# A two-part transformer kernel: sigmoids before a weight copy, a pool mixer on padded buffers, retention products in another order, four banks drained before their second step

## The chip, the core and the metric

The kernel runs as one program on one core of a Trainium2 chip. The core has TensorE (PE, matrix products, with weight loads shown as PEld), VectorE (DVE), ScalarE (ACT), GpSimd (POOL) and SyncE (SP, which issues the DMAs). The metric is device time in microseconds. Before the change, three runs gave 2049.99, 2050.32 and 2055.86 us, median 2050.32 us.

## The reference, cut to what matters

Two blocks follow one another on 512 tokens of width 1024. The first has two hybrid layers, and the change touches only these; the second (attention and a mixture of experts) is left as it was.

```python
def hybrid_layer(x, ...):                      # twice
    h = rms_norm(x, norm_g) * (1.0 + scale) + shift
    pool_u, pool_g, q, k, v, ret_g, rw, rw_g, gate_logits = split(h @ w_in)
    o_pool = causal_pool_mixer(pool_u, pool_w, pool_scale) * silu(pool_g)
    o_ret = retention(q, k, v, positions, ret_norm_g) * silu(ret_g)
    o_rwkv = rwkv7_time_mix(rw, ...) * silu(rw_g)
    y = einsum('btnw,nwd->btnd', stack([o_pool, o_ret, o_rwkv]), w_branch)
    return x + gate * (sum(sigmoid(gate_logits) * y) @ w_out)

def causal_pool_mixer(u, ...):                 # windows 2, 4, 8, 16: one per group of 128 channels
    outs.append(win_sum / count - u)           # count = min(t + 1, w); then a linear map per group

def retention(q, k, v, ...):                   # 4 heads of 128, 4 chunks of 128 tokens
    o = (q k^T * mask) v + q_dec R             # R_next = chunk_decay * R + k_tail^T v

def rwkv7_time_mix(p, ...):                    # r, w, k, v, a from p mixed with the token before
    w = -softplus(-(w0 + tanh(wl) @ w2)) - 0.5;  a = sigmoid(a0 + al @ a2)
    y = head_norm(scan(...)) * ln_w + ln_b + bonus
```

## The kernel before, in words

Every engine has its own instruction list, written out by hand, and engines wait for each other by semaphores. `after(name, k)` is a wait, `inc` lets an instruction count a semaphore up, and `step` does that and waits at once for its own instruction.

Weights come in chunks of 512 KB, loaded by SP into a ring of three (`load_chunks`). A chunk's load is issued when the product that used its place is full. ACT then copies the rounded high part (`high`, L998), POOL subtracts it to get the low part (`low`, L1474), and only then may PE multiply: each product is three passes (high by high, high by low, low by high). One feature job is 24 products of 128 by 512 (L681) and uses one chunk. The projections follow each other as r, wl, k, lora, v, pu, pg, rg, tg and so on, four chunks each.

PE writes into eight PSUM banks in turn. `jobs` lists all products of a layer in PE's order, with the semaphore that tells that the bank is drained; a job must wait until the job eight places before it is drained (`open_bank`).

Four places of a layer matter here, in PE's order.

1. After the job k3, PE makes the small products of the two low-rank maps (z0 to z3 and a0 to a3, L745), then v0 (L681). v0 takes the bank of z0, which ACT drains by the sigmoid at L1026. On ACT, the copy of k3 (L1021) is followed by `high` of the chunk for v1 (L998), and then by the four sigmoids.
2. While PE does pu and pg, POOL runs the pool mixer (L1486 to L1505): per window a number of shifted additions, each with a copy of the first `lag` columns, then the division by the count, the subtraction and a fix of the first 16 columns. Two weight splits follow each window: pg0 and pg1 after window 0, pg2 and pg3 after window 1, rg0 and rg1 after window 2, rg2 and rg3 after window 3.
3. In the same time DVE makes the decay-weighted operands of the time mixing: from the last token mix (L1201) over L1219 to L1249 to the bonus (L1253). PE needs the first of these for its diagonal products dg (L768). The products dg2 take the banks that the bonus instructions drain.
4. In retention PE makes, for each chunk n, the scores of chunk n + 1 (L898), then o (L915 from the masked scores, with L918 from the state between them), then the outer product kv (L925). DVE masks the scores (L1362) and updates the state from kv (L1370, L1374). After that PE transposes the time mixing's output into four banks (ty, L713), makes three gate products (L681), transposes the retention's output (to, L713) and goes on to the next gate product, which takes the bank of ty3. DVE drains each of the four ty banks at L1382 and multiplies by the gate at L1384 before it drains the next.

Of the kernel before, what the change touches and what calls it, by code (L numbers as in the profile page):

```python
# [149 lines left out]
def program(nc, ada, wstream, lparams, gparams, consts, distances, experts, last_norm, x_in, pos_in, out):  # L150
    with ExitStack() as ctx:
# [139 lines left out]
        def job(name, drained, k):  # L291
            jobs.append((name, drained, k))
# [60 lines left out]
        for n in range(NT):  # L353
            if n < NT - 1:
                job(f"sc{n + 1}", "pret_ready", 2 + n)
            job(f"o{n}", "o_ready", 1 + n)
            if n < NT - 1:
                job(f"kv{n}", "R_ready", 1 + n)
# [48 lines left out]
        for name, per in (("bank_full", NJ), ("params_loaded", 16), ("x_done", 8), ("adaload0", 16 * ADA_B // 2), ("adaload1", 16 * ADA_B // 2),  # L407
# [5 lines left out]
                          ("pu_ready", 4), ("pg_ready", 4), ("pool_step", 10 * 2 + 4 * 4), ("pool_d", 4),  # L413
# [234 lines left out]
        def layer_tensor(pe, L):  # L648
# [254 lines left out]
            for n in range(NT):  # L903
# [3 lines left out]
                after("pret_ready", n + 1)  # L907
                if n == 0:
                    after("ret_tok")
                else:  # L910
                    after("R_ready", n)
                o = open_bank(f"o{n}")
                for h in range(RET_H):
                    cols = slice(h * P, h * P + P)
                    mm = nc.tensor.matmul(o[:, cols], p_ret[n % 2][:, cols], rv_tok[:, n, cols],  # L915
                                          start=True, stop=(n == 0))
                    if n > 0:
                        mm = nc.tensor.matmul(o[:, cols], qdT[:, h, t0:t0 + P], state[:, h, :],  # L918
                                              start=False, stop=True)
                full(mm)  # L920
                if n < NT - 1:
                    o = open_bank(f"kv{n}")
                    for h in range(RET_H):
                        cols = slice(h * P, h * P + P)
                        mm = nc.tensor.matmul(o[:, cols], k_tail[:, n, cols], rv_tok[:, n, cols],  # L925
                                              start=True, stop=True)
                    full(mm)

# [49 lines left out]
        def layer_scalar(act, L):  # L978
# [39 lines left out]
            for i, (z, name) in enumerate(((K_, "k"), (V_, "v"))):  # L1018
                for c in range(CW):
# [3 lines left out]
                    high(FIRST[name] + c + RING)  # L1023
                if name == "k":
                    for c in range(CW):
                        inc(nc.scalar.activation(G_[:, c, :], bank(f"z{c}"), ACT.Sigmoid, bias=par("w0", c)), "g_ready")  # L1026
                    for c in range(CW):
# [126 lines left out]
        def layer_vector(dve, L):  # L1154
# [210 lines left out]
            for n in range(NT):  # L1365
                if n < NT - 1:
                    retention_mask(n + 1)
                    o = bank(f"kv{n}")
                    if n == 0:
# [11 lines left out]
            for c in range(CW):  # L1381
                step(v.scalar_tensor_tensor(br_rwkv[:, c, :], bank(f"ty{c}"), par("ln_w", c), br_rwkv[:, c, :], ALU.mult, ALU.add),  # L1382
                     "y_scaled")
# [76 lines left out]
        def layer_gpsimd(pool, L):  # L1460
# [20 lines left out]
            tmp = [zt.rearrange("p u t -> p (u t)")[:, i * T:i * T + T] for i in range(2)]  # L1481
            fix = tt.rearrange("p u t -> p (u t)")[:, 0:16]
# [6 lines left out]
            for i, w in enumerate(WINDOWS):  # L1489
                u = pool_u[:, i, :]  # L1490
                after("pu_ready", i + 1)
                src, lag = u, 1
                while lag < w:
                    dst = tmp[0] if src is not tmp[0] else tmp[1]
                    inc(g.tensor_copy(dst[:, 0:lag], src[:, 0:lag]), "pool_step")
                    count[0] += 1
                    step(g.tensor_tensor(dst[:, lag:T], src[:, lag:T], src[:, 0:T - lag], ALU.add))
                    src, lag = dst, 2 * lag

                step(g.tensor_tensor(fix, src[:, 0:16], con("inv_count")[:, 16 * i:16 * i + 16], ALU.mult))  # L1500
                step(g.tensor_tensor(fix, fix, u[:, 0:16], ALU.subtract))
# [1206 lines left out]
```

## Time and profile before

| what | value |
|---|---|
| median of three runs | 2050.32 us |
| the profiled execution: its own time | 2051.84 us |
| the profiled execution: its span | 2049.4 us |
| PE busy | 1933.6 us, 94% |
| DVE, ACT, POOL busy | 1138.7, 761.1, 693.6 us |
| first layer's PE work | from 44 to 692 us of the span |
| second layer's PE work | from 701 us on |

PE is the engine to watch. A busy PE is not PE at its full clock: the granted clock is listed for stretches. Where a row gives an idle time in brackets, it names what ended it.

### The profile page before, as it was taken

The page shows a single profiled execution, that of the slowest core. Times are in us where ns is not written, and L with a number is a line of the kernel's source. Part 1 is how long each engine was busy: PE and PEld are TensorE (multiplying, and loading weights), DVE is VectorE, ACT ScalarE, POOL GpSimd, SP SyncE. Part 2 cuts the span into 40 slices and gives each one's busy share as a digit, 9 for nine tenths or more (in the row PEclk, how much of TensorE's full clock was granted, in tenths as well). Part 3 has the DMA queues.
Part 4 walks back from the last instruction along what each step waited for, and adds up shares of the span by engine and source line. Part 5 has one row for each costly group of instructions (what it writes and reads, how often), then busy time and mean ns, then how long its engine had stood idle before and what let it go on. Part 6 is the DMA issues. An engine that isn't in the chain of part 4 may idle for free. (4 is left out here: it accounts for less than half of the span.)

```text
span 2049.4 us, 26280 instructions
## 1 busy us (share of the span) xinstructions
PE 1933.6 (94%) x10768; PEld 1565.2 (76%) x10768; DVE 1138.7 (56%) x1425; ACT 761.1 (37%) x1121; POOL 693.6 (34%) x391
## 2 busy tenths in 40 slices
PE   8998999999999899999999999989989898999994
PEld 6777889998888777788998888869868784555552
DVE  5258755556765427766555676442135335666664
ACT  3345210333222343511132322343346645555552
POOL 0458210324444246821142444434410012333330
PEclk8999999999999999999999999989979998999997
DMA  7322300214444332220021554434310067999973
GB/s 312 95 89 75 103 1 1 84 62 154 176 175 154 118 98 84 81 83 1 21 83 62 194 175 156 137 115 159 113 32 2 21 257 275 343 346 357 344 286 132
DMA packets 78143, 284.63 MB, mean 139 GB/s; under 512 B 27284, under 2 KB 27412, under 8 KB 60741
## 3 DMA queue, kind: packets, MB, share of 16 engines
q1 hardware_dynamic: 71140, 272.36, 38.0%
q0 software_dynamic: 6144, 8.40, 1.2%
q8 instruction: 88, 1.44, 0.3%
q10 hardware_dynamic: 736, 2.14, 0.3%
q14 instruction: 35, 0.28, 0.0%
HBM read 274.44 MB, written 23.63 MB: 145 GB/s over the span
## 5 line engine op out<-in xcount | busy, mean ns | idle before, releaser
L1474 POOL TENSOR_TENSOR wmem_r<-wmem,wmem_r 128x1024 fp32r<-128x1024 f32 x170 | 420.4, 2474 | 665.7 <-ACT wmem_r L998 654.7
L681 PE MATMUL banks<-h_hi_r,wmem_r 128*128 128x512 f32 x1632 | 512.8, 394 | 13.5 <-POOL wmem_r L1474 7.7
L681 PEld LDWEIGHTS banks<-h_hi_r,wmem_r 128*128 128x128 f32 x1632 | 309.0, 189 | 82.0 <-POOL wmem_r L1474 9.5
L998 ACT ACTIVATE wmem_r<-wmem 128x1024 fp32r<-128x1024 f32 x170 | 180.2, 1060 | 484.7 <-DMA wmem<-wstream 481.7
L681 PE MATMUL banks<-hT_r,wmem_r 128*128 128x512 f32 x816 | 319.7, 392 | 0.0
L681 PEld LDWEIGHTS banks<-hT_r,wmem_r 128*128 128x128 f32 x816 | 154.7, 190 | 32.4 <-issue 0.5
L2042 PE MATMUL banks<-wmem_r,gm_mem_r 128*80 128x512 f32 x496 | 178.2, 420 | 0.0
L2570 POOL TENSOR_TENSOR wmem_r<-wmem,wmem_r 128x1024 fp32r<-128x1024 f32 x30 | 74.8, 2492 | 235.4 <-ACT wmem_r L2110 235.4
L1714 POOL DMA_INDIRECT y_tok_dram<-ztp,y_idx x32 | 66.4, 2075 | 221.3 <-DVE ztp L2496 214.8
L702 PE MATMUL banks<-wmem_r,h_hi_r 128*128 128x256 f32 x768 | 140.4, 285 | 0.0
L1414 DVE SCALAR_TENSOR_TENSOR ztp<-xT,c_act,ztp 128x256 f32<-128x256 f32 x168 | 126.6, 754 | 6.0
L949 PE MATMUL banks<-slots_r,wmem_r 128*128 128x512 f32 x512 | 127.7, 389 | 0.0
L2483 DVE TENSOR_TENSOR slots_r<-slots,wmem_r 128x1024 fp32r<-128x1024 f32 x102 | 120.0, 1217 | 11.9 <-ACT wmem_r L2216 5.7
L702 PEld LDWEIGHTS banks<-wmem_r,h_hi_r 128*128 128x128 f32 x768 | 120.9, 194 | 0.0
L1850 PE MATMUL banks<-h_hi_r,wmem_r 128*128 128x512 f32 x368 | 116.8, 393 | 0.6 <-DVE hT_r L2383 0.6
L949 PEld LDWEIGHTS banks<-slots_r,wmem_r 128*128 128x128 f32 x512 | 96.1, 188 | 19.9
L702 PE MATMUL banks<-wmem_r,hT_r 128*128 128x256 f32 x384 | 109.3, 285 | 0.0
L2042 PEld LDWEIGHTS banks<-wmem_r,gm_mem_r 128*80 128x80 f32 x496 | 73.4, 148 | 44.4 <-issue 8.7
L2216 ACT ACTIVATE wmem_r<-slots 128x1024 fp32r<-128x1024 f32 x102 | 102.1, 1053 | 2.3 <-PE banks L1997 2.3
L1704 PE MATMUL banks<-slots,gm_mem 128*80 128x512 f32 x216 | 97.1, 592 | 0.4 <-issue 0.4
L1850 PEld LDWEIGHTS banks<-h_hi_r,wmem_r 128*128 128x128 f32 x368 | 69.1, 188 | 16.5 <-DVE hT_r L2383 2.3
L2042 PE MATMUL banks<-slots_r,gm_mem_r 128*80 128x512 f32 x204 | 79.9, 392 | 0.0
(422 smaller groups left out, 3358.0 us busy)
## 6 DMA issues: line engine op xcount, KB each, us to landing
wmem<-wstream SPq DMA_DIRECT2D x206, 512.0 KB, 3.6
slots<-experts SPq DMA_DIRECT2D x80, 1024.0 KB, 6.6
xT<-ada SPq DMA_DIRECT2D x24, 1024.0 KB, 5.8
xT<-experts SPq DMA_DIRECT2D x16, 1024.0 KB
slots<-ada SPq DMA_DIRECT2D x8, 1024.0 KB, 17.8
x_keep<-xT SPq DMA_DIRECT2D x2, 2048.0 KB, 17.6
xT<-x_keep SPq DMA_DIRECT2D x2, 2048.0 KB, 9.2
dil_rows<-dil_once SPq DMA_DIRECT2D x1, 2560.0 KB
```

Of the source, the lines that this page charges most:

```text
L681: mm = nc.tensor.matmul(o, r(lhs[:, k, :]), r(rhs[:, k, :]), start=(k == 0 and i == 0), stop=(k == KD - 1 and i == 2))
L702: mm = nc.tensor.matmul(o[n // 2][:, cols], r(lhs[:, KD // 2 * half + k, n * P:n * P + P]), r(rhs[:, k, :]), start=(half == 0 and n % 2 == ...
L949: mm = nc.tensor.matmul(o, r(lhs[:, i % 2 * CW + k, :]), r(rhs[:, k, :]), start=(k == 0 and j == 0), stop=(k == CW - 1 and j == 2))
L998: inc(nc.scalar.activation(r(chunk(b)[0]), w, ACT.Copy), "w_high")
L1414: step(v.scalar_tensor_tensor(acc, w_k, c_k, acc, ALU.mult, ALU.add), "ada_step")
L1474: inc(g.tensor_tensor(r(lo), lo, r(hi), ALU.subtract), "w_split")
L1704: mm = nc.tensor.matmul(bank[0:SLOT, :], h_t[:, f * SLOT:(f + 1) * SLOT], w[:, f, halves[i]], start=(f == 0), stop=(f == 1))
L1850: mm = nc.tensor.matmul(o, r(lhs[:, k, :]), r(rhs[:, k, :]), start=(k == 0 and i == 0), stop=(k == KD - 1 and i == 2))
L2042: mm = nc.tensor.matmul(banks[0:SLOT, 2 + e % 2], r(lhs[:, cols]), r(rhs[:, kk, :]), start=(half == 0 and kk == 0 and i == 0), stop=(half ...
L2216: nc.scalar.activation(r(raw_hi[g % NHI][:, cols]), raw[j % NRAW][:, cols], ACT.Copy).then_inc(SEM["eh_ready"], 1)
L2483: v.tensor_tensor(r(lo), lo, r(raw_hi[g % NHI][:, cols]), ALU.subtract).then_inc(SEM["el_ready"], 1)
L2570: nc.gpsimd.tensor_tensor(r(lo), lo, r(hi), ALU.subtract).then_inc(SEM["a_split"], 1)
```

## The change

ACT: the copy of v1's weights moves behind the four gate sigmoids, in front of the four others. POOL: the sums run on two buffers with eight zero columns ahead, so that the additions cover all 512 columns and need no copies of first columns (but one of a single column per window), and the splits stand elsewhere between them. PE: kv stands before o, and the four products of o with the state follow the four with the scores, behind their own wait. DVE: the state update waits for o as well, and the four ty banks are drained before the gate products.

```diff
             if n < NT - 1:
                 job(f"sc{n + 1}", "pret_ready", 2 + n)
+                job(f"kv{n}", "R_ready", 1 + n)
             job(f"o{n}", "o_ready", 1 + n)
-            if n < NT - 1:
-                job(f"kv{n}", "R_ready", 1 + n)
...
-                after("pret_ready", n + 1)
                 if n == 0:
                     after("ret_tok")
-                else:
-                    after("R_ready", n)
-                o = open_bank(f"o{n}")
-                for h in range(RET_H):
-                    cols = slice(h * P, h * P + P)
-                    mm = nc.tensor.matmul(o[:, cols], p_ret[n % 2][:, cols], rv_tok[:, n, cols],
-                                          start=True, stop=(n == 0))
-                    if n > 0:
-                        mm = nc.tensor.matmul(o[:, cols], qdT[:, h, t0:t0 + P], state[:, h, :],
-                                              start=False, stop=True)
-                full(mm)
+                head = [slice(h * P, h * P + P) for h in range(RET_H)]
                 if n < NT - 1:
                     o = open_bank(f"kv{n}")
...
                     full(mm)
+                after("pret_ready", n + 1)
+                o = open_bank(f"o{n}")
+                for h, cols in enumerate(head):
+                    mm = nc.tensor.matmul(o[:, cols], p_ret[n % 2][:, cols], rv_tok[:, n, cols],
+                                          start=(h == 0), stop=(n == 0), skip_group_check=True)
+                if n > 0:
+                    after("R_ready", n)
+                    for h, cols in enumerate(head):
+                        mm = nc.tensor.matmul(o[:, cols], qdT[:, h, t0:t0 + P], state[:, h, :],
+                                              start=False, stop=True, skip_group_check=True)
+                full(mm)
...
-                    high(FIRST[name] + c + RING)
+                    if (name, c) != ("k", CW - 1):
+                        high(FIRST[name] + c + RING)
                 if name == "k":
                     for c in range(CW):
                         inc(nc.scalar.activation(G_[:, c, :], bank(f"z{c}"), ACT.Sigmoid, bias=par("w0", c)), "g_ready")
+                    high(FIRST["k"] + CW - 1 + RING)
...
                     o = bank(f"kv{n}")
+                    after("bank_full", JOB[f"o{n}"] + 1)
...
             for c in range(CW):
-                step(v.scalar_tensor_tensor(br_rwkv[:, c, :], bank(f"ty{c}"), par("ln_w", c), br_rwkv[:, c, :], ALU.mult, ALU.add),
-                     "y_scaled")
+                inc(v.scalar_tensor_tensor(br_rwkv[:, c, :], bank(f"ty{c}"), par("ln_w", c), br_rwkv[:, c, :], ALU.mult, ALU.add),
+                    "y_scaled")
+            for c in range(CW):
+                after("y_scaled", c + 1)
                 inc(v.scalar_tensor_tensor(br_rwkv[:, c, :], br_rwkv[:, c, :], par("ln_b", c), rg_gate[:, c, :], ALU.add, ALU.mult),
                     "rwkv_done")
...
+            def window_sums(i):
+
+                u = pool_u[:, i, :]
+                after("pu_ready", i + 1)
+                dst, other = padded
+                inc(g.tensor_copy(dst[:, PAD:PAD + 1], u[:, 0:1]), "pool_step")
+                count[0] += 1
+                step(g.tensor_tensor(dst[:, PAD + 1:], u[:, 1:T], u[:, 0:T - 1], ALU.add))
+                lag = 2
+                while lag < WINDOWS[i]:
+                    step(g.tensor_tensor(other[:, PAD:], dst[:, PAD:], dst[:, PAD - lag:PAD - lag + T], ALU.add))
+                    dst, other, lag = other, dst, 2 * lag
+                summed[i] = dst[:, PAD:]
+
+            def window_rest(i):
+
+                u, src = pool_u[:, i, :], summed[i]
+                inc(g.tensor_tensor(fix, src[:, 0:16], con("inv_count")[:, 16 * i:16 * i + 16], ALU.mult), "pool_step")
+                count[0] += 1
+                step(g.tensor_scalar(src[:, 16:], src[:, 16:], 1.0 / WINDOWS[i], None, ALU.mult))
+                step(g.tensor_tensor(u[:, 16:], src[:, 16:], u[:, 16:], ALU.subtract))
+                inc(g.tensor_tensor(u[:, 0:16], fix, u[:, 0:16], ALU.subtract), "pool_d")
...
+            low(FIRST["pg"], FIRST["pg"] + 1)
+            window_sums(0)
+            low(FIRST["pg"] + 1, FIRST["pg"] + 2)
+            window_rest(0)
+            low(FIRST["pg"] + 2, FIRST["rg"])
+            window_sums(1)
+            window_rest(1)
+            window_sums(2)
+            window_rest(2)
+            low(FIRST["rg"], FIRST["rg"] + 2)
+            window_sums(3)
+            window_rest(3)
+            low(FIRST["rg"] + 2, FIRST["tg"])
```

How this moves instructions is shown at two places. The first is POOL in a layer, from the end of the splits up to pu3 (the row with x17) on; `wmem_r<-wmem,wmem_r` is a split, `ztp` holds the mixer's sums and `gm_mem` its input. Before:

```order
L1474 TENSOR_TENSOR wmem_r<-wmem,wmem_r 128x1024 x17
L1495 COPY ztp<-gm_mem 128x1
L1497 TENSOR_TENSOR ztp<-gm_mem 128x511
L1500 TENSOR_TENSOR ztp<-ztp,cst 128x16
L1501 TENSOR_TENSOR ztp<-ztp,gm_mem 128x16
L1502 TENSOR_SCALAR ztp<-ztp 128x512
L1503 TENSOR_TENSOR gm_mem<-ztp,gm_mem 128x512
L1504 COPY gm_mem<-ztp 128x16
L1474 TENSOR_TENSOR wmem_r<-wmem,wmem_r 128x1024 x2
L1495 COPY ztp<-gm_mem 128x1
L1497 TENSOR_TENSOR ztp<-gm_mem 128x511
```

The same place on POOL in the changed kernel:

```order
L1476 TENSOR_TENSOR wmem_r<-wmem,wmem_r 128x1024 x17
L1518 MEMSET ztp 128x8 x2
L1476 TENSOR_TENSOR wmem_r<-wmem,wmem_r 128x1024
L1493 COPY ztp<-gm_mem 128x1
L1495 TENSOR_TENSOR ztp<-gm_mem 128x511
L1476 TENSOR_TENSOR wmem_r<-wmem,wmem_r 128x1024
L1505 TENSOR_TENSOR ztp<-ztp,cst 128x16
L1507 TENSOR_SCALAR ztp<-ztp 128x496
L1508 TENSOR_TENSOR gm_mem<-ztp,gm_mem 128x496
L1509 TENSOR_TENSOR gm_mem<-ztp,gm_mem 128x16
L1476 TENSOR_TENSOR wmem_r<-wmem,wmem_r 128x1024 x2
L1493 COPY ztp<-gm_mem 128x1
```

The splits of pg0 and pg1 moved into window 0, and those of pg2 and pg3 (the last row with x2) moved ahead of window 1.

The second place is PE in retention, after the first two scores; `slots,wu_sb` are the products with masked scores, `state,slots` those with the state, and plain `slots` the outer products kv. Before:

```order
L915 MATMUL banks<-slots,wu_sb 128x128 [waits kT_ready,ret_tok,pret_ready]
...
L925 MATMUL banks<-slots 128x128 [waits kT_ready]
...
L898 MATMUL banks<-slots,gm_mem 128x128 [waits kT_ready]
...
L915 MATMUL banks<-slots,wu_sb 128x128 [waits kT_ready,R_ready,pret_ready]
L918 MATMUL banks<-state,slots 128x128
```

The same place on PE in the changed kernel:

```order
L912 MATMUL banks<-slots 128x128 [waits kT_ready,ret_tok]
...
L917 MATMUL banks<-slots,wu_sb 128x128 [waits kT_ready,pret_ready]
...
L897 MATMUL banks<-slots,gm_mem 128x128 [waits kT_ready]
...
L912 MATMUL banks<-slots 128x128 [waits kT_ready]
...
L917 MATMUL banks<-slots,wu_sb 128x128 [waits ret_tok,pret_ready]
...
L922 MATMUL banks<-state,slots 128x128 [waits R_ready]
...
```

The outer products moved ahead of o, and the wait for the state moved from before all eight products of o to before its last four.

## Rows read from the trace of the kernel before

**Rows 1.** The page: busy time, share of the span and instructions of each engine.

```profile
PE 1933.6 (94%) x10768; PEld 1565.2 (76%) x10768; DVE 1138.7 (56%) x1425; ACT 761.1 (37%) x1121; POOL 693.6 (34%) x391
```

**Rows 2.** Waits of PE: who was waited for, us in total, times, longest.

```profile
PE banks L811 <- DVE gm_mem L1282: 10.8, 14, 1.2
...
PE banks L681 <- POOL wmem_r L1474: 7.7, 2, 4.0
...
PE banks L768 <- DVE slots L1253: 3.8, 2, 2.1
...
PE banks L681 <- DVE slots L1382: 3.0, 2, 1.5
PE banks L681 <- ACT slots L1026: 2.7, 2, 1.4
```

**Rows 3.** Timeline of PE, layer 1: start, us, instruction [idle before <-releaser].

```profile
102.35 0.47 PE L681 MATMUL banks<-h_hi_r,wmem_r 128*128 128x512 f32 x1 [1.33 <-ACT slots L1026]
...
165.82 0.80 PE L681 MATMUL banks<-h_hi_r,wmem_r 128*128 128x512 f32 x1 [3.75 <-POOL wmem_r L1474]
...
186.63 2.95 PE L768 MATMUL banks<-slots 64*128 64x128 f32 x32 [1.73 <-DVE slots L1253]
...
439.99 0.46 PE L915 MATMUL banks<-slots,wu_sb 128*128 128x128 f32 x2 [1.02 <-issue]
...
463.40 0.47 PE L681 MATMUL banks<-h_hi_r,wmem_r 128*128 128x512 f32 x1 [1.52 <-DVE slots L1382]
```

**Rows 4.** Stretches: us; busy of PE, PEld, DVE, ACT, POOL; PEclk, DMA share, GB/s.

```profile
102.30:125.80 23.50, 23.45 (x96) 19.27 (x97) 2.25 (x3) 10.14 (x14) 8.84 (x5) 0.93 0.26 88
760.20:782.00 21.80, 21.74 (x96) 18.06 (x97) 2.25 (x3) 10.17 (x14) 8.60 (x5) 1.00 0.27 94
165.80:171.20 5.40, 5.38 (x13) 4.22 (x14) 5.40 (x6) 1.00 (x1) 5.27 (x6) 0.50 0.01 2
186.60:191.60 5.00, 4.94 (x42) 4.58 (x43) 2.07 (x4) 4.33 (x14) 4.94 (x6) 0.66 0.33 56
427.40:441.90 14.50, 13.36 (x115) 12.86 (x114) 5.21 (x13) 3.33 (x5) 4.00 (x2) 1.00 0.12 37
```

**Rows 5.** Timeline of ACT, layer 1, ahead of v0.

```profile
99.15 1.06 ACT L998 ACTIVATE wmem_r<-wmem 128x1024 fp32r<-128x1024 f32 x1 [2.86 <-DMA wmem<-wstream]
...
101.52 0.69 ACT L1026 ACTIVATE slots<-banks,lpar 128x512 f32<-128x512 f32 x1
```

**Rows 6.** Timeline of DVE, layer 1: first and last step of the chain.

```profile
126.81 0.75 DVE L1201 SCALAR_TENSOR_TENSOR slots<-banks,lpar,slots 128x511 f32<-128x511 f32 x1 [4.69 <-ACT slots L1021]
...
185.21 1.87 DVE L1253 TENSOR_TENSOR slots<-banks,slots 128x512 f32<-128x512 f32 x3
```

**Rows 7.** Lines of DVE, 126 to 188 us: busy, mean ns, idle before.

```profile
L1247 DVE TENSOR_TENSOR slots<-slots 128x2048 f32<-128x2048 f32 x1 | 3.4, 3356 | 0.0
...
L1242 DVE TENSOR_TENSOR slots<-slots 128x2048 f32<-128x2048 f32 x1 | 3.1, 3085 | 0.0
...
L1246 DVE SCALAR_TENSOR_TENSOR slots<-slots 128x2048 f32<-128x2048 f32 x1 | 2.7, 2699 | 0.0
...
L1244 DVE TENSOR_TENSOR slots<-slots 128x2048 f32<-128x2048 f32 x1 | 2.3, 2292 | 0.4 <-ACT slots L1044 0.4
```

**Rows 8.** Timeline of POOL, layer 1, in the same stretch.

```profile
174.94 3.60 POOL L1502 TENSOR_SCALAR ztp<-ztp 128x512 f32<-128x512 f32 x1
...
178.62 2.31 POOL L1503 TENSOR_TENSOR gm_mem<-ztp,gm_mem 128x512 f32<-128x512 f32 x1
```

**Rows 9.** Timeline of DVE and POOL, layer 1, retention and after it.

```profile
439.01 0.88 DVE L1374 SCALAR_TENSOR_TENSOR state<-state,banks 128x128 f32<-128x128 f32 x4 [2.28 <-PE banks L925]
...
459.71 0.75 DVE L1382 SCALAR_TENSOR_TENSOR slots<-banks,lpar,slots 128x512 f32<-128x512 f32 x1
...
459.54 2.51 POOL L1474 TENSOR_TENSOR wmem_r<-wmem,wmem_r 128x1024 fp32r<-128x1024 f32 x1 [1.74 <-ACT wmem_r L998]
```

**Rows 10.** The line L1382: duration ns min/median/max, first and last start us, forms.

```profile
L1382 DVE SCALAR_TENSOR_TENSOR slots<-banks,lpar,slots x8: 736/743/752, 455.2 to 1116.7; 128x512 f32<-128x512 f32 x8
```

More of the change, by code:

```diff
@@ L412, in program @@
                           ("k_mod", 2), ("rk_ready", 1), ("kk_unit", 2), ("bonus_ready", 4),
[L413 removed]
+                          ("pu_ready", 4), ("pg_ready", 4), ("pool_step", 2 + 4 + 10 + 4 * 3), ("pool_d", 4),
                           ("pool_done", 4), ("g_sum", 1), ("g_prev", 1), ("exp_prev", 1), ("exp_plus", 1),
@@ L906, in layer_tensor @@
                     retention_scores(n + 1)
-                after("pret_ready", n + 1)
                 if n == 0:
                     after("ret_tok")
-                else:
-                    after("R_ready", n)
-                o = open_bank(f"o{n}")
-                for h in range(RET_H):
-                    cols = slice(h * P, h * P + P)
-                    mm = nc.tensor.matmul(o[:, cols], p_ret[n % 2][:, cols], rv_tok[:, n, cols],
-                                          start=True, stop=(n == 0))
-                    if n > 0:
-                        mm = nc.tensor.matmul(o[:, cols], qdT[:, h, t0:t0 + P], state[:, h, :],
-                                              start=False, stop=True)
-                full(mm)
+                head = [slice(h * P, h * P + P) for h in range(RET_H)]
                 if n < NT - 1:
                     o = open_bank(f"kv{n}")
[L923 to L926, printed above, removed]
+                    for cols in head:
+                        mm = nc.tensor.matmul(o[:, cols], k_tail[:, n, cols], rv_tok[:, n, cols], start=True, stop=True)
                     full(mm)
+                after("pret_ready", n + 1)
[9 more added lines that the diff above has]
+                full(mm)
             after("y_norm")
@@ L1479, in step @@
                 after("pool_step", count[0])
-            tmp = [zt.rearrange("p u t -> p (u t)")[:, i * T:i * T + T] for i in range(2)]
-            fix = tt.rearrange("p u t -> p (u t)")[:, 0:16]
+            PAD = max(WINDOWS) // 2
+            padded = [flat_ztp[:, i * (PAD + T):(i + 1) * (PAD + T)] for i in range(2)]
+            fix = flat_ztp[:, 2 * (PAD + T):2 * (PAD + T) + 16]
+            summed = {}
+            def window_sums(i):
[17 more added lines that the diff above has]
+                inc(g.tensor_tensor(u[:, 0:16], fix, u[:, 0:16], ALU.subtract), "pool_d")
             low(0, 2)
@@ L1488, in layer_gpsimd @@
                 pool.wait_ge(SEM["const_rest"], 16)
[L1489 to L1501, printed above, removed]
-                step(g.tensor_scalar(src, src, 1.0 / w, None, ALU.mult))
-                step(g.tensor_tensor(u, src, u, ALU.subtract))
-                inc(g.tensor_copy(u[:, 0:16], fix), "pool_d")
-                low(FIRST["pg"] + 2 * i, FIRST["pg"] + 2 * i + 2)
+            for a in padded:
+                inc(g.memset(a[:, 0:PAD], 0.0), "pool_step")
+                count[0] += 1
+            low(FIRST["pg"], FIRST["pg"] + 1)
[11 more added lines that the diff above has]
+            low(FIRST["rg"] + 2, FIRST["tg"])
             low(FIRST["tg"], FIRST["pool_w"])
```

## The prediction

> **What bounds the kernel now.** I read the busy times first: PE is busy for 94% of the span [rows 1], so little is to be had in all, and only where PE stands still or runs at a lower clock. Then the waits of PE [rows 2]. The group at the top, the masked Gram products at L811, is not touched. The change is aimed at the next ones: the weight split of POOL, 7.7 us in two waits (one in each layer), DVE's bonus 3.8, DVE's bank drain L1382 3.0 and ACT's sigmoid L1026 2.7. The timeline of PE [rows 3] gives the wait of layer 1 in each, and the rest is layer 2's: 1.33 and 1.4 us at L1026, 3.75 and 4.0 at the split, 1.73 and 2.1 at the bonus, 1.52 and 1.5 at L1382, and 1.02 before the last o of retention (taken alike in layer 2, whose instructions are the same). Last, the stretches [rows 4], for the clock: behind 1.33 us of idling in layer 1, v0 to v3 took 23.5 us at a mean granted clock of 0.93; the same 96 products took 21.8 us at 1.00 in layer 2. So the lower level (1.2 GHz instead of 2.4) cost 1.7 us there. After the split wait, 5.4 us ran at 0.50 throughout, which costs half, 2.7 us; after the bonus wait, 5.0 us at 0.66, that is 1.7 us.
>
> **Part 1, sigmoids ahead of the copy.** ACT idled 2.86 us for the chunk of v1 and copied it for 1.06 us, and only then came the sigmoid's table load (the 1.3 us between the two rows) and the first sigmoid at 101.52 [rows 5]. v0 needs the bank of z0, so it waited for just this. With the sigmoids ahead, the 2.86 us of idling take in the table load, and the first bank is free some 3 us before PE asks. The copy for v1 then comes after four sigmoids of 0.69 us, about 1 us later than before, and v1 is a whole job (21.8/4 = 5.4 us) behind v0, so nothing waits for it. v0 starts 1.33 us earlier in layer 1, and without the idling I expect no fall of the clock: 1.7 more. So v3 ends 3.0 us earlier in layer 1 and 1.4 in layer 2.
>
> **Part 2, the pool mixer.** The splits for pg2 and pg3 stood behind window 1, and PE stood still for 3.75 us until 165.8 [rows 3]. Now they come ahead of window 1, behind the rest of window 0 alone, and I estimate that the wait shrinks to 1.5 us or less. But what is late next? DVE works from the last token mix at 126.81 to the bonus at 185.21 [rows 6] with 0.4 us idle in its own lines [rows 7], and dg2 starts when the second bonus bank is drained. That chain starts with v3 and does not ask POOL for anything. PE will therefore pass pg2 earlier and wait longer in front of dg: the 3.75 us with its 2.7 us of clock, and 4.0 in layer 2, buy nothing. What counts is by how much the chain itself moves: 3.0 and 1.4 us earlier by part 1, and what POOL does to it.
>
> POOL does something. DVE's additions of 128x2048 take 2.29 us undisturbed (L1244); L1242 took 3.09, L1246 2.70 and L1247 3.36 [rows 7]. POOL's subtraction L1503 took 2.31 us and its scaling L1502 3.60 in the same stretch [rows 8]. The two engines take turns there: whichever comes second waits. The six large two-operand steps of the chain lost 3.9 us in this way (0.8, 0.4 and 1.1 by these rows, the other two, L1232 and L1233, about 0.8 each like L1242). In the new order POOL comes to the stretch with window 2's full additions (about 1.1 us each) instead of 16-column pieces, of which DVE notices nothing. Laying the two lists side by side in turns, I get 0.4 less at L1233, 0.5 less at L1242 and 1.0 to 1.6 more on the next four: the chain ends 0.7 us later in each layer. Bounds: no collision at all would save 3.4 us (3.9 less the wait for ACT that then shows); two steps meeting a split of 2.4 us and four meeting additions of 1.1 would lose 9.2 instead of 3.9, 5.4 more. I take 0.7, from the turns.
>
> The Trainium skill (SBUF — State Buffer, "SBUF: two separate sides" and "Who interferes with whom") says that a DVE instruction with two SBUF inputs and a GpSimd one that reads SBUF exclude each other, for the whole instruction of the one that started first. For POOL's two-operand steps the rows agree: L1247, which met the subtraction, lost 1.1 us, its whole length. For the one-operand scaling they do not: L1246 met it for 1.4 us and lost 0.4. By the rule as stated, the scaling would cost DVE 1.0 us more in each layer.
>
> Then the clock: PE now stands still in front of dg for some 7 us in two pieces, not 1.7. I take the 2.7 us of the stretch at 0.50 instead of 1.7: 1.0 worse per layer (0 to 1.3).
>
> **Part 3, stateless products first.** Retention took 14.50 us, of which PE was busy for 13.36 [rows 4]: 1.14 us of waits, 1.02 of them before the last o, for the state. The state update is 0.88 us long [rows 9] and now starts after o of the chunk before, a group of eight passes later. A group takes 13.36/14 = 0.95 us, and o's four score products now cover the update. So 1.0 us comes free in each layer; if the cover falls short by the semaphore's way, 0.6.
>
> **Part 4, banks drained in one go.** The gate product at 463.40 waited 1.52 us for the fourth drain L1382, which stood behind three gate steps L1384. Drained in a row at 0.75 us each from 455.2 on [rows 10], the fourth bank is free at 458.2, before the transposes are done (463.4 less the wait, 461.9). A split by POOL does not hold a drain up: the drain at 459.71 took 0.75 us beside a split from 459.54 to 462.05 [rows 9]; it reads one operand from PSUM. So 1.5 us comes free in each layer. What is late next is the split of that gate product's own weights, but the split at 459.54 is already that of the product after it. Both parts fall in a stretch where PE has no other wait until the end of the layer, and so they count in full.
>
> **Sum.** Layer 1: -3.0 + 0.7 + 1.0 - 1.0 - 1.5 = -3.8. Layer 2: -1.4 + 0.7 + 1.0 - 1.0 - 1.5 = -2.2. Together -6.0 us, from 2051.84 to 2045.8 in the profiled execution's terms. That execution was 1.5 us above the median of the runs, so I forecast 2050.32 - 6.0 = 2044.3 us.
>
> **Rivals.**
> - *DVE's chain loses its collisions.* Less POOL work in all, and window 2's work may fall into the scans, which show no loss. Against it: five of the six steps stand close together and POOL has work all the time. With 3.4 us saved instead of 0.7 lost in each layer: 2044.3 - 8.2 = 2036.1. Chance 0.08.
> - *DVE's chain collides more.* The full additions of window 2 and the two splits for rg0 and rg1 come down on the six steps. At the bound, 5.4 instead of 0.7 in each layer: 2044.3 + 9.4 = 2053.7, slower than before. It decides from 3.7 us more than I take per layer. For it: POOL's full additions are now bunched. Against: most collisions of before were with pieces as long. Chance 0.10.
> - *Retention's wait only changes its place.* The update now waits for o as well; if cover and signal times leave 1.0 us standing, part 3 gives nothing: 2046.3. Against it: the cover of 0.95 is longer than the update. Chance 0.10.
> - *POOL's scaling blocks DVE in full*, 1.0 more per layer by its own length: 2046.3. Against it is the 0.4 of L1246. Chance 0.10. (This is the skill's rule above.)
>
> **How the numbers follow.** My own forecast has 0.62; by itself it spans 2040 to 2048.5, with the bounds of the clock and 1.5 us either way for the collisions. A change under 0.3%, some 6.1 us, can't be told from none here, and the forecast of 6.0 lies at this border, so its chance halves: a little under one half faster. With the first rival and a small part of the last two, faster has 0.45; the rest of the forecast, the last two and most of the second rival make 0.50 the same; 0.05 is left for slower by more than that. The range, 2037.5 to 2051, takes in nearly all of the first rival's way and half of the second's.
>
> **What would show it right or wrong.** Right: no wait of PE for L1026 and L1382; v0 to v3 in 21.8 us in both layers; the wait for POOL's split at 1.5 us or gone; in its place PE waiting 6 to 8 us in front of dg for L1246 and L1253, in two pieces, with the clock at 0.50 behind it; the chain of DVE still 59 to 61 us long; retention in about 13.5 us. Wrong: a total wait in front of dg as short as before with the split's wait gone (then DVE did not bound), DVE's steps at 2.29 us (first rival) or above 3.4 us throughout (second), or a wait of 1 us for the state left in retention.

## The result and the profile after

The changed kernel takes 2043.45 us, the median of 7 runs (2036.99 to 2049.43), against 2050.32 of 7 runs of the kernel before: 0.995 of it, with an interval of 0.993 to 0.997. By that ratio the gain is 10 us (6 to 14), by the two medians 6.9. The forecast was 2044.3. The profiled execution took 2043.71 us, its span 2041.2. One run of the kernel before, beside the last four experiments, took 2987.17 us at a mean granted clock of 0.60, and no number here includes it.

The page's busy times of the changed kernel, and below them PE's waits (who was waited for, us in total, times, longest):

```profile
PE 1930.9 (95%) x10768; PEld 1565.5 (77%) x10768; DVE 1138.5 (56%) x1425; ACT 761.2 (37%) x1121; POOL 686.9 (34%) x375
```

```profile
PE banks L810 <- DVE gm_mem L1281: 10.8, 14, 1.2
...
PE banks L767 <- DVE slots L1252: 7.6, 2, 4.3
...
PE banks L767 <- DVE slots L1245: 2.5, 2, 2.2
...
PE banks L680 <- POOL wmem_r L1476: 2.1, 3, 0.9
...
PE banks L767 <- ACT gm_mem L1035: 1.8, 1, 1.8
```

Against [rows 2], the waits for the sigmoid and for the bank drain are gone, the split fell from 7.7 to 2.1, and the waits in front of dg rose from 3.8 to 11.9: for the bonus (L1252), for the product that makes the rows of ar (L1245) and, in layer 2, for ACT's silu of pg2, which stands behind the exps and frees a bank. Layer 1 waits 6.5 us there in two pieces, layer 2 5.3 in three (0.27 for L1245, 1.77 for the silu, 3.28 for the bonus). So 5.6 us went from the split's line and 8.1 came to dg's. PE's busy time hardly moved. (Line numbers are a few lower than before: L767 was L768, L680 was L681, L1252 was L1253.)

PE's timeline in layer 1 (start, us, instruction, idle before it):

```profile
102.65 0.50 PE L680 MATMUL banks<-h_hi_r,wmem_r 128*128 128x512 f32 x1
...
161.77 0.50 PE L680 MATMUL banks<-h_hi_r,wmem_r 128*128 128x512 f32 x1 [0.94 <-POOL wmem_r L1476]
...
178.60 2.27 PE L767 MATMUL banks<-slots 64*128 64x128 f32 x32 [2.23 <-DVE slots L1245]
185.16 3.79 PE L767 MATMUL banks<-slots 64*128 64x128 f32 x32 [4.28 <-DVE slots L1252]
...
437.12 1.06 PE L917 MATMUL banks<-slots,wu_sb 128*128 128x128 f32 x8
438.01 1.06 PE L922 MATMUL banks<-state,slots 128*128 128x128 f32 x8
438.90 1.06 PE L917 MATMUL banks<-slots,wu_sb 128*128 128x128 f32 x8
440.11 1.16 PE L922 MATMUL banks<-state,slots 128*128 128x128 f32 x8
```

These answer to [rows 3]: v0 starts with no wait (102.65), pg2 waits 0.94 instead of 3.75, and dg waits in two pieces, 2.23 and 4.28, where it had one of 1.73. Compare starts, too: groups of eight start 0.89 us apart, though a row says 1.06, because the end of the last product is modelled. So a bracket behind such a group shows a stop 0.17 us too short (by the same comparison, 0.25 behind the transposes ahead of the gate product); this will be needed below. Only in front of the last four state products (440.11) is there a gap, 1.21 instead of 0.89.

The stretches that answer to [rows 4] (us; busy of PE, PEld, DVE, ACT and POOL; granted clock, DMA share, GB/s):

```profile
102.60:124.60 22.00, 22.00 (x98) 18.15 (x98) 2.55 (x4) 8.70 (x12) 10.16 (x5) 1.00 0.30 96
...
161.70:167.10 5.40, 5.33 (x23) 4.43 (x24) 5.40 (x6) 1.06 (x1) 5.24 (x7) 1.00 0.31 97
185.10:190.10 5.00, 4.94 (x38) 4.75 (x39) 2.10 (x4) 2.53 (x7) 4.84 (x5) 0.50 0.25 43
```

```profile
428.20:441.10 12.90, 12.75 (x114) 12.56 (x113) 5.22 (x13) 3.33 (x5) 3.99 (x2) 1.00 0.13 42
```

v0 to v3 run at 2.4 GHz throughout, and so does the stretch behind the pg2 wait of 0.94 us. Behind dg's two stops of 2.23 and 4.28 us the clock is at 1.2 GHz for the whole stretch (0.50), where it had a mean of 0.66 behind the one stop of 1.73 in the kernel before. Retention takes 12.9 us instead of 14.5.

ACT ahead of v0, with DVE's and POOL's steps in the chain that bounds dg2, from their timelines:

```profile
98.00 1.28 ACT L1024 ACT_TABLE_LOAD   x1
99.30 2.42 ACT L1024 ACTIVATE slots<-banks,lpar 128x512 f32<-128x512 f32 x4
101.60 1.07 ACT L995 ACTIVATE wmem_r<-wmem 128x1024 fp32r<-128x1024 f32 x1
```

```profile
125.57 0.75 DVE L1200 SCALAR_TENSOR_TENSOR slots<-banks,lpar,slots 128x511 f32<-128x511 f32 x1 [4.69 <-ACT slots L1018]
...
172.48 3.02 DVE L1243 TENSOR_TENSOR slots<-slots 128x2048 f32<-128x2048 f32 x1 [0.33 <-ACT slots L1043]
175.43 3.12 DVE L1245 SCALAR_TENSOR_TENSOR slots<-slots 128x2048 f32<-128x2048 f32 x1
178.47 3.12 DVE L1246 TENSOR_TENSOR slots<-slots 128x2048 f32<-128x2048 f32 x1
181.52 2.29 DVE L1248 TENSOR_TENSOR slots<-slots 128x2048 f32<-128x2048 f32 x1
183.74 2.47 DVE L1252 TENSOR_TENSOR slots<-banks,slots 128x512 f32<-128x512 f32 x4
```

```profile
159.20 4.98 POOL L1476 TENSOR_TENSOR wmem_r<-wmem,wmem_r 128x1024 fp32r<-128x1024 f32 x2
...
173.43 6.01 POOL L1498 TENSOR_TENSOR ztp<-ztp 128x512 f32<-128x512 f32 x2
...
181.64 3.48 POOL L1507 TENSOR_SCALAR ztp<-ztp 128x496 f32<-128x496 f32 x1
```

The sigmoids start at 99.30 instead of 101.52 [rows 5], and the weight copy follows them. DVE's chain from the last token mix to the bonus lasts 58.2 us (125.57 to 183.74), where it lasted 58.4 [rows 6]: it only starts earlier. POOL has both splits at 159.20 and window 2's two additions beside three of DVE's products. The two take turns: the products take 3.0 to 3.1 us each instead of 2.29, and the additions 3.0 instead of 1.04.

What each step of a layer gave, by the starts of PE's first matmuls in it, in us, before and after:

| stretch | layer 1 | layer 2 |
|---|---|---|
| a product of the r job (58.60 and 711.95 us after) to the end of v3 | 68.84, 65.99 | 67.24, 66.11 |
| end of v3 to dg2 | 60.80, 60.58 | 60.59, 59.42 |
| dg2 to rg0 (the clock) | 9.11, 9.89 | 8.93, 9.71 |
| rg0 to the start of retention | 231.67, 233.14 | 229.91, 229.93 |
| retention | 14.45, 12.92 | 14.45, 12.92 |
| its end to the gate product | 21.55, 19.78 | 21.55, 19.77 |
| to the layer's output | 185.0, 185.0 | 185.0, 185.0 |

Without the fourth row, which the change does not touch, this is 5.6 less in layer 1 and 4.8 in layer 2, 10.4 in all. The span fell by 8.2: the fourth row took 1.5 back, the set-up ahead of layer 1 began its products 1.6 us later, and 0.9 us less was spent between and behind the layers.

### The profile page after: what moved, and what is told of

Same layout as the page of the kernel before. It is cut to its first block and busy times, and to the rows that moved or that the text cites. A ratio compares the mean times of both kernels' runs of the same rounds, so it can differ in the third digit from the quotient of the medians.

```text
span 2041.2 us, 26273 instructions
## 1 busy us (share of the span) xinstructions
PE 1930.9 (95%) x10768; PEld 1565.5 (77%) x10768; DVE 1138.5 (56%) x1425; ACT 761.2 (37%) x1121; POOL 686.9 (34%) x375
## 5 line engine op out<-in xcount | busy, mean ns | idle before, releaser
L1476 POOL TENSOR_TENSOR wmem_r<-wmem,wmem_r 128x1024 fp32r<-128x1024 f32 x170 | 413.6, 2434 | 665.6 <-ACT wmem_r L995 654.6
L680 PE MATMUL banks<-h_hi_r,wmem_r 128*128 128x512 f32 x1632 | 508.7, 391 | 2.2 <-POOL wmem_r L1476 2.1
L680 PEld LDWEIGHTS banks<-h_hi_r,wmem_r 128*128 128x128 f32 x1632 | 306.4, 188 | 69.3 <-POOL wmem_r L1476 3.8
L680 PE MATMUL banks<-hT_r,wmem_r 128*128 128x512 f32 x816 | 317.6, 389 | 0.0
L680 PEld LDWEIGHTS banks<-hT_r,wmem_r 128*128 128x128 f32 x816 | 153.2, 188 | 31.7 <-issue 0.5
L2597 POOL TENSOR_TENSOR wmem_r<-wmem,wmem_r 128x1024 fp32r<-128x1024 f32 x30 | 74.7, 2490 | 235.1 <-ACT wmem_r L2137 235.1
```

What stands on the lines that cost most here:

```text
L680: mm = nc.tensor.matmul(o, r(lhs[:, k, :]), r(rhs[:, k, :]), start=(k == 0 and i == 0), stop=(k == KD - 1 and i == 2))
L1476: inc(g.tensor_tensor(r(lo), lo, r(hi), ALU.subtract), "w_split")
L2597: nc.gpsimd.tensor_tensor(r(lo), lo, r(hi), ALU.subtract).then_inc(SEM["a_split"], 1)
```

## The experiments

All times are medians in us; the ratio is against the kernel before on the same chip. That had 2051.43 (30 runs) beside the first four, 2052.11 (17) beside the next four and 2052.32 (22) beside the last four.

| run | what | median (runs) | ratio, 95% interval |
|---|---|---|---|
| e1 | sigmoids alone | 2048.26 (11) | 0.9983, 0.9968 to 0.9998 |
| e2 | pool mixer alone | 2057.37 (6) | 1.0040, 1.0022 to 1.0058 |
| e3 | retention alone | 2045.44 (12) | 0.9973, 0.9957 to 0.9990 |
| e4 | drains alone | 2046.61 (12) | 0.9976, 0.9958 to 0.9993 |
| e5 | changed, pool mixer of before | 2039.62 (6) | 0.9941, 0.9921 to 0.9961 |
| e6 | changed, windows 1 to 3 after DVE's chain | 2050.55 (12) | 0.9991, 0.9975 to 1.0007 |
| e7 | changed, DVE's chain cut | 2026.17 (6) | 0.9885, 0.9858 to 0.9912 |
| e8 | as e7, pool mixer of before | 2037.32 (6) | 0.9926, 0.9901 to 0.9952 |
| e9 | changed, again | 2040.30 (12) | 0.9947, 0.9928 to 0.9966 |
| e10 | as e5, again | 2038.51 (6) | 0.9939, 0.9919 to 0.9959 |
| e11 | as e2, again | 2054.34 (12) | 1.0014, 0.9998 to 1.0029 |
| e12 | as e7, exps left behind pg1 | 2032.76 (6) | 0.9918, 0.9896 to 0.9940 |

**The four parts, each alone on the kernel before.** Each takes its own part of the diff: e1 the lines of ACT, e2 POOL's, e3 those of retention on PE and DVE, e4 DVE's drains.

> The kernel before with the sigmoids ahead of the weight copy, and nothing else. Theory (DVE's chain starts with v3 and sets when dg2 may start): v0 no longer waits, v3 ends about 2.9 us earlier after r2 in layer 1 (1.3 of idling, the rest clock) and 1.2 in layer 2, and dg2 moves with it, since the chain of DVE does; the wait for POOL's split stays at 3.7 to 4.0 us. Time about 4 us under before, 2046. Rival (POOL sets the pace of pu and pg, so what is won at v0 is waited off at the split): wait at the split 5 us or more, time as before, 2050.

> The kernel before with the new pool mixer and its place between the splits, and nothing else. Theory: the wait for the split falls from 3.75 and 4.0 us to about 1, the waits in front of dg0 and dg2 grow by as much, and the time from the products kss to dg2 stays what it was within 1.5 us in each layer, because DVE's chain is 57 to 59 us long whatever PE does. Time 2048 to 2051. Rival (the split bounded): dg2 comes 5 us earlier in each layer, time 2040 or less. Second rival (more collisions of POOL with DVE): chain longer by over 1 us in each layer, time over 2052.

> The kernel before with the order of products in retention, and nothing else. Theory (both the wait for the state and a part of each wait on a bank go): retention from the first scores to the transposes 12.9 us instead of 14.45 in each layer, time about 3 us under before, 2047. Rival (what it wins is waited off at the gate product that needs ty3's bank, since its drain comes later in DVE's order): that wait grows from 1.5 to 2.5 us or more, and the time falls by 1 us or less.

> The kernel before with the four ty banks drained in one go, and nothing else. Theory: the wait of 1.5 us at the fourth gate product is gone in both layers, 1.5 to 1.8 us between the transposes ty and that product, nothing given back before the end of the layer; time about 3.5 us under before, 2047. Rival (the gate steps, now later, hold up the retention branch's products): a new wait in the products of the branches at L949, time as before.

With the sigmoids alone, v0 to v3 takes 21.94 us in both layers and dg2 starts 61.0 and 60.5 us behind v3, as before (60.8 and 60.6): what is gained ahead of v3 reaches dg2 whole. The median fell by 3.2 us, where I had expected 4; with retention alone it fell by 6.0 (expected 3) and with the drains alone by 4.8 (expected 3.5). With the pool part alone, the waits are moved and not taken away:

```profile
PE banks L768 <- DVE slots L1253: 6.5, 2, 3.3
...
PE banks L768 <- DVE slots L1246: 2.5, 2, 2.2
PE banks L681 <- POOL wmem_r L1474: 2.1, 2, 1.1
PE banks L768 <- ACT gm_mem L1036: 1.8, 1, 1.8
```

The split has 2.1 us and dg 10.8, and dg2 starts 60.7 and 59.5 us behind v3. These starts fit the theory. The median, 5.9 us over the kernel before, I did not expect: it is the time of the second rival, but without the rival's mechanism, since dg2 does not come later. Retention alone is 12.92 us long in both layers, and with the drains alone the stretch behind it takes 19.77: the same numbers as in the whole change. These two act by themselves and for the whole layer. The four ratios add up to -5.7 us against -10.3 for the whole; with e11's in place of e2's it is -11.

**The pool part taken out of the change (e5), and the last products of DVE's chain freed of POOL (e6).** e5 has the sums, copies and splits of POOL as before, all else as changed. e6:

```diff
-            low(FIRST["pg"] + 2, FIRST["rg"])
+            low(FIRST["pg"] + 2, FIRST["rg"] + 1)
+            after("bonus_ready", CW)
+            low(FIRST["rg"] + 1, FIRST["rg"] + 2)
             window_sums(1)
             window_rest(1)
             window_sums(2)
             window_rest(2)
-            low(FIRST["rg"], FIRST["rg"] + 2)
             window_sums(3)
```

> The changed kernel with the pool mixer put back to the form of before (sigmoids, retention and drains as changed). Theory, that the split wait lies beside DVE's chain: the wait for POOL's first scaling is back at 3.7 to 4.0 us in each layer with the clock drop behind it, and the last wait for dg shrinks by as much, so the distance from the end of v3 to the start of dg2 is what it was in the changed kernel (58.4 and 57.2 us) less 0 to 1.5 us in each layer for the collisions; TensorE is slow in the stretch before dg and whole in the one behind dg2. Time 2041 to 2045 us where the changed kernel has 2043.5. First rival, that the pool part is worth its 3 us a layer after all: 2049 to 2051. Second rival, from the run of the pool part alone, which was 6 to 8 us over the kernel before: the pool part costs that here too, and the time falls to 2036 or 2037.

> The changed kernel, but POOL does the splits pg2 to rg0 at once, then waits until DVE's last product of the chain, and only then sums windows 1 to 3. POOL shares nothing with DVE's products and scans of the chain. Theory, that DVE's longer products there come from POOL's window sums beside them: the products that took 3.0 to 3.2 us take 2.29, the scans 12.5 instead of 12.8, the chain from v3 is 2.4 us shorter in each layer, dg2 starts 2 to 3 us earlier in each, and the time is 2037 to 2040. Rival, that the longer products come from ACT's exps or from nothing that POOL does: the durations stay within 0.1 us and the time within 1.5 us of the changed kernel's 2043.5. Second rival: the pool product needs window 3 early, and the wait comes back in front of it: the wait is seen there and the time is 2045 or more.

e5 has the split wait back at 3.76 and 3.66 us, and dg2 is 60.8 and 60.2 us behind v3, against 60.6 and 59.4 in the changed kernel. So 2.8 us of waiting for POOL in each layer are worth 0.2 and 0.8 at dg2, and the clock behind dg2 takes that back (dg2 to rg0 9.1 and 7.5 us, against 9.9 and 9.7). I expected the distance to be a little shorter here, and it was a little longer; the time, 2039.6, fell between the theory's and the second rival's.

In e6 DVE's rows show what POOL did to it (DVE's timeline, layer 1):

```profile
171.34 2.29 DVE L1241 TENSOR_TENSOR slots<-slots 128x2048 f32<-128x2048 f32 x1
174.85 2.29 DVE L1243 TENSOR_TENSOR slots<-slots 128x2048 f32<-128x2048 f32 x1 [1.22 <-ACT slots L1043]
177.06 2.28 DVE L1245 SCALAR_TENSOR_TENSOR slots<-slots 128x2048 f32<-128x2048 f32 x1
179.26 2.28 DVE L1246 TENSOR_TENSOR slots<-slots 128x2048 f32<-128x2048 f32 x1
181.47 2.28 DVE L1248 TENSOR_TENSOR slots<-slots 128x2048 f32<-128x2048 f32 x1
```

With POOL standing still, all five take 2.29 us, and dg2 comes 2.1 and 2.4 us earlier behind v3 than in the changed kernel. The cause is POOL, then, and part of the gain goes to a wait for ACT's exp (1.22).

The sixteen scans at the chain's middle (L1238) still stand beside POOL's splits in e6, and they show a larger loss, which the prediction read as none (DVE's and POOL's timelines, layer 1):

```profile
164.07 2.55 DVE L1238 TENSOR_TENSOR_SCAN slots<-cst,slots 128x128 f32<-128x128 f32 x1
166.55 0.39 DVE L1238 TENSOR_TENSOR_SCAN slots<-cst,slots 128x128 f32<-128x128 f32 x1
```

```profile
163.83 2.52 POOL L1476 TENSOR_TENSOR wmem_r<-wmem,wmem_r 128x1024 fp32r<-128x1024 f32 x1
```

A scan beside a split takes 2.5 us. From 166.35 to 167.53 POOL does nothing; there a scan takes 0.39 us, and the next one starts 0.31 us later. Sixteen such scans would take about 5.1 us, an estimate from these two figures. They took 13.2 us in the kernel before, 12.8 in the changed one and 13.0 in e6 (where I had expected 12.5). So POOL costs the scans some 8 us in each layer in all three kernels, twice what the six large products lost in the kernel before (3.9). No run here tried to take that away, so how much of it would reach dg2 is not shown.

In e6 the time did not follow dg2, since the splits for the next products now stand behind three windows (PE's and POOL's timelines):

```profile
211.65 0.80 PE L680 MATMUL banks<-h_hi_r,wmem_r 128*128 128x512 f32 x1 [6.51 <-POOL wmem_r L1476]
```

```profile
209.03 5.02 POOL L1476 TENSOR_TENSOR wmem_r<-wmem,wmem_r 128x1024 fp32r<-128x1024 f32 x2
```

From rg0 to the end of the diagonal sums, the two layers lost 8.8 and 10.6 us. I had expected a wait at the pool product in the bad case; it came at rg2, whose split is the first of the two at 209.03.

**DVE's chain cut (e7), and the same without the pool part (e8).** ACT takes the inverse square root as an exponential of a logarithm, in place of ACT's square root and DVE's reciprocal of 12.9 us, and ACT's exps of the decay come one product earlier (the lines left out change only semaphore counts):

```diff
-            inc(nc.scalar.activation(X2[:, :, :], X2[:, :, :], ACT.Sqrt), "kss_sqrt")
+            inc(nc.scalar.activation(X2[:, :, :], X2[:, :, :], ACT.Ln), "kss_sqrt")
+            after("kss_sqrt", 1)
+            inc(nc.scalar.activation(X2[:, :, :], X2[:, :, :], ACT.Exp, scale=-0.5), "kss_sqrt")
...
-                if c == 1:
+                if c == 0:
...
-            step(v.reciprocal(X2[:, :, :], X2[:, :, :]), "kk_unit")
```

> The changed kernel with DVE's chain cut: the norm's inverse square root is taken by ACT as a logarithm and an exponential (two instructions of about 2.9 us) in place of ACT's square root and DVE's reciprocal of 13 us, and ACT's three exps of the decay stand behind pg0 and not behind pg1. What bounds dg2 by the theory is then gone: DVE's chain ends some 13 us earlier, before TensorE comes to dg. Theory: no wait for DVE stands in front of dg0 to dg2 in either layer, each layer is 5.5 to 7.5 us shorter, the clock drop behind dg2 goes (0.8 each), and the time is 2027 to 2032. Rival, that behind DVE's chain stands ACT's chain or the transfer of the gathered diagonals: a wait of 2 to 6 us remains in front of dg, for ACT or for a DMA, and the time is 2037 to 2041. Second rival, that the waits are set by POOL: the waits stay as long as they are, and the time is within 2 us of 2043.5.

> The same shortened chain, with the pool mixer in the form of before. Theory, that the pool part of the change is only hidden behind DVE's chain: with the chain short, the wait for POOL's first scaling (3.7 to 4.0 us in each layer, and some 2 us in each for the clock behind it) ends last again, and this kernel is 9 to 12 us slower than its neighbour with the padded sums: 2037 to 2043. Rival, that the split wait is worth nothing wherever it stands: both kernels within 2 us of each other.

PE in e7, from the bonus sums on (timeline, layer 1), and in e8 the two waits for the split (likewise):

```profile
173.01 3.59 PE L758 MATMUL banks<-slots,cst 128*128 128x512 f32 x8
176.53 3.84 PE L767 MATMUL banks<-slots 64*128 64x128 f32 x64
```

```profile
151.85 0.50 PE L680 MATMUL banks<-h_hi_r,wmem_r 128*128 128x512 f32 x1 [2.18 <-POOL wmem_r L1477]
...
165.40 0.50 PE L680 MATMUL banks<-h_hi_r,wmem_r 128*128 128x512 f32 x1 [0.72 <-POOL wmem_r L1477]
```

In e7 all 64 products of dg stand in one row, with no wait in either layer; behind dg2 the clock is whole, and dg2 comes 52.4 us behind v3 in both, 8.2 and 7.0 earlier than in the changed kernel. DVE still waits 2.71 us for ACT's exp in this chain. Two things were changed at once here; e12 below takes them apart. e7 is also faster than both kernels: 2026.17, a little under what I expected, and 0.9885 of the kernel before. With the pool mixer of before, dg2 comes 57.6 us behind v3, 5.2 later, in each layer; the medians lie 11.2 apart. The pool part is worth 5 us a layer as soon as the reciprocal and the late exps are out of its way. I had expected the wait of e8 in one piece of 3.7 to 4.0; it came in two, 2.18 and 0.72, and most of the rest is the clock behind the first (a mean of 0.69 over the next 5.5 us, which costs 1.7).

**The pairs again (e9 to e11), and the short chain with late exps (e12).** e9 is the changed kernel, e10 is e5 and e11 is e2. e12 is e7 but for this:

```diff
-                if c == 0:
+                if c == 1:
```

> The changed kernel itself, beside the two runs that follow, on one chip: what the pool part is worth is read from this kernel and the next, and from the third and the kernel before. Theory: the pool part moves TensorE's stop from pg2 to dg and takes no time off the way from v3 to dg2; the one longer stop in front of dg leaves a slow stretch behind dg2 in both layers. So it costs 2 to 6 us in both pairs: 2043 to 2045 here, some 4 more than the next. Rival: the two differences seen so far are scatter between jobs, and here the pairs agree within 1.5 us.

> The changed kernel with the pool mixer of before. Theory (the pool part costs 2 to 6 us where DVE's chain is long): 2038 to 2041, some 4 us under the changed kernel. Rival: within 1.5 us of it.

> The kernel before with the pool part alone. Theory (the pool part costs 2 to 6 us where DVE's chain is long): 2053 to 2057, and the profile has more slow stretches around dg2 or behind it than the kernel before. Rival: within 1.5 us of the kernel before.

> The changed kernel with the inverse square root by ACT's logarithm and exponential as in the run with the short chain, but ACT's three exps of the decay left behind pg1. It tells whether DVE's chain alone bounded dg2, or ACT's exps stand right behind it. Theory: with DVE's 13 us gone the exps behind pg1 end last; a wait for DVE's products that follow the exps (the ones for bk and ar), or for ACT, of 2 to 5 us in each layer stays in front of dg, and the time is 2032 to 2038. Rival: the exps behind pg1 are early enough, no wait stays and the time is that of the short chain, 2026 to 2028.

With the pool part, the changed kernel is 1.8 us slower than without it, and the kernel before 2.0 us slower with it. Both differences point the same way as e2's 5.9, but they are hardly over what I had set for scatter (1.5): e9's runs spread over 16 us, its interval overlaps e10's, and e11's takes in 1. So the pool part gains nothing in these two kernels. That it costs something is clear of the noise in e2 alone, and not settled. e10's waits, against those of the changed kernel:

```profile
PE banks L680 <- POOL wmem_r L1476: 7.6, 2, 3.8
...
PE banks L767 <- DVE slots L1252: 4.7, 2, 2.6
```

These are 12.3 us in all, where the changed kernel has 14.0 on the same lines (2.1, 7.6, 2.5 and 1.8), and 13.4 in e9.

In e12 the reciprocal alone is gone, and dg2 comes 56.8 us behind v3 in both layers, 3.8 and 2.6 earlier than in the changed kernel. The edit touches only this step and ACT's two in its place, so this shows the chain to be what bounded dg2. One wait in front of dg2 remains, 3.84 us in layer 1:

```profile
182.91 1.44 PE L767 MATMUL banks<-slots 64*128 64x128 f32 x10 [3.84 <-DVE slots L1253]
```

dg0 to dg2 takes 6.3 us instead of e7's 1.9, in both layers. DVE now stands idle for 8.55 us for ACT's exp. So behind DVE's reciprocal ACT's exps stand next, 4.4 us a layer, and e7's second edit takes these away (6.6 us between the medians, which were taken on two chips; 6.8 by the ratios).

## Why the forecast held, step by step

- **DVE's chain bounds dg2** (part 2's first claim): right. The wait moved from the split to dg, in two pieces of 2.23 and 4.28 us in layer 1. In layer 2 it is 5.3 us in three, one of them for ACT's silu, where I had 6 to 8 in two. The chain stayed 58.2 and 57.0 us long, under the 59 to 61 that I had named. That it bounds is shown by e12, and e7 and e8 show the pool part's gain appearing when the chain is cut.
- **Sigmoids**, -3.0 and -1.4: measured -2.85 and -1.13. The fall of the clock ahead of v3 is gone, as forecast; 21.94 us for the stretch, where I had 21.8.
- **The chain's collisions**, +0.7 a layer: wrong in sign, -0.2 and -1.2. This is the largest miss, 2.8 us of the sum. The taking of turns was right (e6 takes POOL away, and the steps are at 2.29), but my laying of the two lists side by side put it on too many steps. The four steps from L1243 on lost 0.9 us more than before in layer 1 and 0.2 in layer 2; I had counted 1.0 to 1.6, and my sum took the upper end. In layer 1 L1248 met only the scaling, which came second and did not hold it up; in layer 2 L1243 and L1245 kept to 2.30 and 2.28. The step at L1233 gained 0.9 in both layers (counted: 0.4), the one at L1242 nothing (counted: 0.5), and the scans, which I left out, 0.35.
- **The clock behind dg2**, +1.0 a layer: measured +0.8 in both, and as much in e9 (9.71 and 9.69 us from dg2 to rg0). Its size is a matter of the execution, too: in e2, with stops of 2.24 and 3.25 us in layer 1 and the same three as here in layer 2, the stretch took 8.91 and 8.83.
- **Retention**, -1.0 a layer: measured -1.53. The step that failed is reading the gain from one bracket of 1.02 us. The prediction's 0.95 us for a group is 0.89 by the starts. So that stop cost 0.17 more, and smaller gaps between groups, which carry no bracket, went too: 14 groups at 0.89 us are 12.47 of the 12.92 us, so 0.45 us of gaps is left of 2.0.
- **Drains**, -1.5 a layer: measured -1.77, for the same reason (the bracket of 1.52 was 0.25 short). DVE drains all four banks in one row of 2.73 us, and PE has no wait there.

```profile
454.44 2.73 DVE L1382 SCALAR_TENSOR_TENSOR slots<-banks,lpar,slots 128x512 f32<-128x512 f32 x4
```

The forecast sum was -6.0, and the same steps measured -10.4: 2.8 from the chain, 1.1 from retention, 0.5 from the drains, and 0.4 each way from the sigmoids and the clock. The medians of the first runs lie 6.9 apart, nearer to the forecast than its steps are; the ratio, and e9 with 12.0 between the medians and 0.9947, put the gain at the steps' 10. So the time came out close partly by chance.

Of the rivals, more collisions (+9.4) and the retention wait that only moves are out by the rows. Fewer collisions is nearest to what layer 2 did, with about a third of the saving it gave; its bound of 3.4 us counted six products and none of the scans' 8. The scaling that blocks DVE in full is out for this order: L1248 took 2.29 us beside it (181.64), and it is the scaling that took 3.48 us, where it took 1.45 in e6 with DVE idle. Here the scaling came second. In e7 it is DVE's step L1249 that came second, behind a scaling that had itself waited for DVE's step before (timelines, layer 1):

```profile
170.81 3.48 POOL L1508 TENSOR_SCALAR ztp<-ztp 128x496 f32<-128x496 f32 x1
```

```profile
172.90 2.68 DVE L1249 TENSOR_TENSOR slots<-slots 128x2048 f32<-128x2048 f32 x1
```

L1249 started with 1.39 us of the scaling left and took 0.4 us longer than 2.29, as L1246 did before the change [rows 7]. So the rival is out in this order, too.

What stays open is where the pool part's cost lies. In the profiles of e9 and e10 dg2 comes 0.2 and 0.9 us earlier behind v3 with the pool part, and the clock behind dg2 costs 0.8 more in each layer: about 0.5 us in all. The two spans differ by 6.8 us, but 2.8 of that lie ahead of layer 1's products and 3.6 behind the layers, where the pool part does nothing. Another 0.4 us lies outside the span (run time less span is 2.5 us in e9 and 2.1 in e10). So the profiles of this pair show a cost of 1 us at most, and e2's 5.9 stays unexplained.

## What to carry to other kernels

Before a wait is taken away, find the chain that ends at the next meeting of the engines; if it does not ask the engine that was waited for, the wait will only move there, and may take the clock with it. To see whether an edit is worthless or only hidden, cut the other chain and measure with and without it: the same pool edit gave nothing in the one kernel (1.8 us slower, hardly clear of the scatter) and 11.2 us in the other. Read a stop from the starts on both sides of it: the bracket was short, and small gaps without brackets added as much again. And compare each group of instructions with its own undisturbed time: the scans looked whole at 13.2 us, and some 8 of them were POOL's.

## What the runs showed of the hardware

The same kernel does not have the same clock in each execution. In the changed kernel, the stretch from the diagonal sums to retention's projections, which no part of the change touches, took 106.3 us in one execution and 103.65 in the other (windows of the first profile and of e9's):

```profile
247.18:353.50 106.32, 100.11 (x898) 96.78 (x897) 57.80 (x85) 11.62 (x18) 14.74 (x18) 0.97 0.01 1
```

```profile
248.40:352.05 103.65, 97.44 (x898) 94.09 (x897) 57.81 (x85) 11.63 (x18) 14.75 (x18) 1.00 0.01 1
```

The instructions are the same, and the granted clock is 0.97 in one and 1.00 in the other. A single profile can therefore not decide an effect of 3 us; a step's own starts can, since between the two executions each stretch from v0 to dg2 and retention agreed within 0.2 us.

The other surprise is that a stop in two pieces of 2.23 and 4.28 us left PE at 1.2 GHz for the whole of the next 5 us, while behind one of 0.94 us it ran at 2.4 GHz (1.00). In e2, stops of 2.24 and 3.25 us were followed by a mean of 0.66 over as long.
